# Row layout of the expert weights in SBUF: each partition's runs of 16 and 8 KB become runs of 8 and 4 KB

## The reference: what is computed

```python
x = x + merged @ w_out
return x + _moe(_rmsnorm(x, g_ffn), w_router, b_router, w_gu, b_gu, w_down, b_down)

# in _moe, for each block of tokens of expert e (top 4 of 32 experts per token):
hgu = tok[rows] @ w_gu[e] + b_gu[e]            # (tokens, 1024) @ (1024, 2048)
gate = jnp.minimum(hgu[:, 0::2], SWIGLU_LIMIT)
up = jnp.clip(hgu[:, 1::2], -SWIGLU_LIMIT, SWIGLU_LIMIT)
act = (up + 1.0) * (gate * jax.nn.sigmoid(SWIGLU_ALPHA * gate))
y = act @ w_down[e] + b_down[e]                # (tokens, 1024) @ (1024, 1024)
```

## Time and profile before

| | us |
|---|---|
| median of 3 runs | 1409.31 |
| lowest, highest | 1408.23, 1413.07 |
| the profiled execution | 1413.07 |
| its span, first to last instruction | 1411.3 |
| PE busy | 1320.6 (94%) |
| DVE busy, ACT busy | 282.4, 252.9 |
| DMA: moved, mean rate | 455.91 MB, 323 GB/s |

### The profile page before, as it was taken

The page is one execution under the profiler, slowest core; times in us unless marked ns, Lnnn a source line. Parts: engine busy times, 40 slices in busy tenths (PEclk is TensorE's granted clock), DMA queues, the critical chain, the costliest instruction groups (busy, mean ns, idle before and its releaser), DMA issues.

```text
span 1411.3 us, 15917 instructions
## 1 busy us (share of the span) xinstructions
PE 1320.6 (94%) x6068; PEld 623.2 (44%) x6069; DVE 282.4 (20%) x832; ACT 252.9 (18%) x515; POOL 24.7 (2%) x36
## 2 busy tenths in 40 slices
PE   5999999989969999999999999999999999999998
PEld 3574767877543343333333433333333333333332
DVE  2243434443141111111011111020111101111011
ACT  1115332344020111101101111011111110111111
POOL 2100000000000000000000000000000000000000
PEclk9999999999989999999999999999999999999999
DMA  9832137321398799995957999999999999999991
GB/s 317 316 123 90 60 132 279 127 71 68 119 360 369 327 425 427 423 427 221 388 231 304 427 426 424 427 426 426 427 423 426 426 427 427 424 425 428 427 420 79
DMA packets 63509, 455.91 MB, mean 323 GB/s; under 512 B 4964, under 2 KB 10232, under 8 KB 30680
## 3 DMA queue, kind: packets, MB, share of 16 engines
q1 hardware_dynamic: 62436, 453.50, 78.1%
q0 software_dynamic: 656, 1.46, 0.4%
q10 hardware_dynamic: 388, 0.55, 0.1%
HBM read 454.45 MB, written 1.05 MB: 323 GB/s over the span
## 4 chain that ended last, share of the span: by engine, by line
PE 54%; DMA 15%; ACT 2%; issue 1%; DVE 0%; SPq 0%; DVEq 0%; ACTq 0%
PE bank L930 26%; PE bank L960 15%; DMA ring<-in_w_down 15%; PE bank L901 4%; PE bank L917 3%; PE bank L893 3%; ACT mq L1222 1%; PE bank L949 1%; ACT sp_ L1212 1%; PE bank L987 0%; PE bank L848 0%; DVE sc L1603 0%; PE bank L836 0%; PE bank L874 0%; PE bank L878 0%
## 5 line engine op out<-in xcount | busy, mean ns | idle before, releaser
L930 PE MATMUL bank<-ring,sp_ 128*64 128x512 f32 x2176 | 481.1, 600 | 0.0
L930 PEld LDWEIGHTS bank<-ring,sp_ 128*64 128x64 f32 x2176 | 154.7, 138 | 324.1 <-issue 324.1
L960 PE MATMUL bank<-ring,mq 128*64 128x512 f32 x1088 | 245.8, 602 | 33.6 <-ACT mq L1222 24.5
L960 PEld LDWEIGHTS bank<-ring,mq 128*64 128x64 f32 x1088 | 76.9, 138 | 179.1 <-issue 154.7
L1646 DVE TENSOR_SCALAR sp_<-bank 128x256 f32<-128x256 f32 x68 | 28.6, 420 | 570.1 <-PE bank L930 570.1
L531 PE MATMUL bank<-ring 128*128 128x512 f32 x288 | 124.8, 593 | 3.1 <-DVE ring L1482 1.6
L1218 ACT ACTIVATE sp_<-sp_ 128x256 f32<-128x256 f32 x68 | 28.4, 418 | 510.1 <-DVE sp_ L1646 510.1
L652 PE MATMUL bank<-ring 128*128 128x256 f32 x448 | 99.4, 381 | 1.5 <-DVE sp_ L1493 1.5
L652 PEld LDWEIGHTS bank<-ring 128*128 128x128 f32 x448 | 84.2, 190 | 13.7 <-issue 2.5
L531 PEld LDWEIGHTS bank<-ring 128*128 128x128 f32 x288 | 54.4, 190 | 69.8 <-issue 67.7
L1662 DVE TENSOR_SCALAR sp_<-cst,rank_it,w_it 128x64 f32<-128x64 f32 x68 | 16.7, 312 | 280.5 <-PE bank L930 280.5
(11 more groups left out here) (289 smaller groups left out, 760.7 us busy)
## 6 DMA issues: line engine op xcount, KB each, us to landing
ring<-in_w_gu SPq DMA_DIRECT2D x128, 2048.0 KB, 25.0
ring<-in_w_down SPq DMA_DIRECT2D x64, 2048.0 KB, 16.4
ring<-in_w_in SPq DMA_DIRECT2D x13, 2048.0 KB, 11.4
ring<-in_w_mem_kv SPq DMA_DIRECT2D x2, 2048.0 KB, 10.1
ring<-in_w_out SPq DMA_DIRECT2D x2, 2048.0 KB, 8.9
ring<-in_cmp_w_k SPq DMA_DIRECT2D x1, 2048.0 KB, 8.2
ring<-in_cmp_w_v SPq DMA_DIRECT2D x1, 2048.0 KB, 9.2
ring<-in_w_br_mem SPq DMA_DIRECT2D x1, 2048.0 KB, 7.5
```

The costliest lines, as they stand in the source:

```text
L930: mm = nc.tensor.matmul(BH[b][64 * hh:64 * hh + 64, :], xgT[:, k, 64 * par:64 * par + 64], w[:, c, o:o + 512], start=False, stop=k == KT - ...
L960: mm = nc.tensor.matmul(BG[64 * hh:64 * hh + 64, :], actT[:, o:o + 64], w[:, c, 512 * hh:512 * hh + 512], start=k == 0, stop=k == KT - 1, ...
```

## The change

Both weight matrices are laid out in the plain way, row 128c+p on partition p. A chunk of `w_gu` becomes two runs of 8 KB per partition, a chunk of `w_down` four runs of 4 KB; either chunk is one contiguous stretch of 2 MB in HBM. `norm_row` then writes `x2` in its own order, and the transposes read neighbouring columns. Every chunk has the bytes, the slot, the semaphore and the place in SP's order that it had, and no matmul changes.

```diff
         def load_chunk(sp, e, q, odd):
             if q < 4:
-                n, src = 2, w_gu[e].rearrange("(p c) n -> p c n", p=P)[:, 2 * q:2 * q + 2, :]
+                n, src = 2, w_gu[e].rearrange("(c p) n -> p c n", p=P)[:, 2 * q:2 * q + 2, :]
             else:
-                n, src = 2, w_dn[e].rearrange("(c p two) n -> p c (two n)", p=P, two=2)[:, 2 * (q - 4):2 * (q - 4) + 2, :]
+                n, src = 4, w_dn[e].rearrange("(c p) n -> p c n", p=P)[:, 4 * (q - 4):4 * (q - 4) + 4, :]
...
                 for q in range(4):
-                    a = act_sb[:, 256 * (q // 2):256 * (q // 2) + 256].rearrange("p (f two) -> p f two", two=2)[:, :, q % 2]
-                    mm = nc.tensor.transpose(BX[:, P * q:P * q + P], a, ident)
+                    mm = nc.tensor.transpose(BX[:, P * q:P * q + P], act_sb[:, P * q:P * q + P], ident)
...
             def norm_row(i):
-                step(V.scalar_tensor_tensor(out=x2[:, i, :].rearrange("p (c d) -> p d c", c=KT),
-                                            in0=x_sb[:, i, :].rearrange("p (d c) -> p d c", c=KT),
-                                            scalar=st[:, 12 + i:13 + i], in1=g_ffn.rearrange("p (d c) -> p d c", c=KT),
+                step(V.scalar_tensor_tensor(out=x2[:, i, :], in0=x_sb[:, i, :], scalar=st[:, 12 + i:13 + i], in1=g_ffn,
                                             op0=ALU.mult, op1=ALU.mult), "x2_ready")
```

## The result

| | before | after |
|---|---|---|
| median, us | 1408.77 (4 runs, 1406.78 to 1413.07) | 1420.89 (4 runs, 1418.84 to 1421.86) |
| profiled execution: span, time | 1411.3, 1413.07 | 1418.2, 1419.95 |

The ratio is 1.0081 (95% interval 1.0059 to 1.0102). A second comparison on another occasion gave 1.0054 (1.0037 to 1.0070); the two intervals together reach from some 5 to 14 us. One execution of the kernel before in the second comparison took 2815.1 us and is not counted. The forecast was 1417, with a range of 1407 to 1423.

What follows compares the result with a forecast made beforehand. PE was taken to pace the work until 757 us, the unpausing DMA stream after that; +9.3 (packets) - 0.75 (norm_row) - 0.8 (transposes) = +7.7 us against the median 1409.31 gave 1417.0, range 1407 to 1423.

Steps and rivals of the forecast that it cites:

- the forecast's own case: Extra packets slow the expert weight stream, partly offset by cheaper norm_row and transposes: +7.7 us, 1412 to 1420, chance 0.56.
- the dearer rival: Expert weight stream: short packets cost what a lone 2 MB load shows, 0.80 us per expert, +14.4 us, 1423.7; chance 0.14.
- The stream sets the end, and only from 757 us on: Mixture of experts: PE paces until SP's last pause ends at 757.28 us, then the full DMA queue, 29.90 us per expert.
- 64 more packets, times a price, times 20 periods: Expert weight loads: 64 more packets per engine and expert at 7.3 ns, 0.47 us, over 20 periods: +9.3 us (0 to +16).
- The 2 KB row's 9.3 ns: Trunk loads of 2 KB runs at 387 GB/s: 9.3 ns per extra packet against 16 KB, used only as support.
- Hidden packets: Rival on the expert weight stream: overlap hides the extra packets, leaving only PE and DVE savings, -1.6 us, 1407.7; chance 0.20.
- Contiguous is faster: Rival: `w_gu` chunks, becoming contiguous in HBM, stream faster; at most 17.4 us, 1390.3 with savings, half-way 1399; chance 0.10.
- The lone load's rate: Rival: 4 KB runs stream at the 400 GB/s of a lone 2 MB load, 0.80 us per expert, 1423.7; chance 0.14.
- The check of the period: Packet times per expert sum to 29.5 us, plus 0.31 on the bias row's engine: 29.8 against the chain's 29.90.
- norm_row: DVE before the experts: unit steps cut the first call from 1.97 to 1.22 us, giving 0.75; the second call gives nothing.
- Transposes: PE weight loads fall from 207 to 142 ns: 0.065 us per item for 12 items before 757 us, 0.8 us (0 to 3.1).
- The signs to look for: Profile after: period about 30.4 us, rate 415 to 421, DMA waits before 1043.55, last pause's end within 3 us of 757.

## Why the prediction was right, and where it was off

- *The number.* 1420.89 lies in the range, but above the 1412 to 1420 that the forecast's own case was given, in the part that was there for the dearer rival. By the traces the change costs +12.2 - 1.4 = +10.8 us, where +7.7 was forecast; that the second comparison's ratio comes to +7.6 us is chance.
- *The stream sets the end, and only from 757 us on.* Shown, with one word to correct: the pause is the DMA engines' last, not SP's. T0 to T1 carries the loss in every trace but those of the shortest packets, which lose some before T0 too. T1 to the end is 42.2 to 43.8 us in the twelve traces, 43.8 before and 43.7 after; the five at 42.2 to 42.5 have TensorE at the lower clock for half as long there. In the kernel before, the slow last down-projection costs 9.97 - 7.29 = 2.7 us, not the 2.9 of the prediction.
- *64 more packets, times a price, times 20 periods.* The mechanism held; the price was the term that was mis-sized: 7.3 ns were forecast, 9.1 to 10.0 measured, so +12.2 us instead of +9.3. The 7.3 came from two rates that the windows give in whole GB/s: with 428 and 423 each off by half a unit, 612.5 and 309.9 ns move by 0.7 and 0.4, and two halves less a whole by 1.4; that a window cuts a few hundred packets comes on top. So rounding alone could hide a price of 8.7 ns. The 2 KB row's 9.3 ns, seven packets more against the same rounding (0.2 ns each), was the one to take; that it agrees to the tenth with the cut into 2 KB is partly luck. The estimate of 3.5 ns from the page "DMA: Bandwidth & Descriptors" of the Trainium skill (section "Why small descriptors are slow (HBM only)") is below what any of the six kernels shows (9.1 ns at the least).
- *Hidden packets* is excluded by the cut at unchanged addresses, 616.0 us for 610.2. *Contiguous is faster* is excluded by the run with only `w_gu` changed, whose chunks become contiguous: 616.1, as much as with the same number of packets at the old addresses. *The lone load's rate* (0.80 us per expert) is too dear: the period rose by 0.60.
- *The check of the period.* The prediction added up 29.5 us for the packets and 0.31 for the engine with the bias row, 29.8, close to 29.90. Spreading the row gave back 0.18, so this agreement was in part luck.
- *norm_row.* 1.28 us against a forecast of 1.22, so 0.69 and not 0.75 is given, and the second call's share did vanish in the wait for PE (1.00 us before L1625).
- *Transposes.* The weight loads fell to a median of 141 ns:

```profile
L948 PEld LDWEIGHTS bank<-cst,sp_ x136: 137/141/230, 435.5 to 1398.4; 128*128 128x128 f32 x136
```

The early items show what that is worth. Ten items of the kernel before take 733.53 - 450.70 = 282.83 us from up-projection to up-projection, ten of the kernel after 728.48 - 446.23 = 282.25, 0.06 us per item, as forecast. Below, rows of before and then after:

```profile
733.53 13.88 PE bank L930 x64
```

```profile
446.23 13.88 PE bank L930 x64
...
728.48 13.88 PE bank L930 x64
```

- *The signs to look for.* Rate 418 (415 to 421 was given), period 30.50 (about 30.4), waits from 952 us. One sign was badly set: a pause that ends more than 3 us elsewhere was to speak against the prediction, and it ended 5.1 us earlier. 3.8 of it came from the trunk, which the change does not touch. A moment that hangs on everything before it is no test; a distance between two events behind the change is.

What stays open: the comparisons of medians lie 3.4 us apart (+12.1 and +8.7 us) though T0 to T1 agrees within 0.3 us, and the +10.8 us of the traces lies above the second interval (5.2 to 9.9 us). Part of it is the granted clock. In the second comparison the 17 executions of the kernel before have a mean of 0.9846 and the ten of the kernel after 0.9859, and within one kernel the time falls by some 1.1 us for each 0.001 (before: 1416.29 us at 0.982, 1408.78 at 0.989). The means lie 8.4 us apart; at equal clock, an estimate, it would be 9.8. For the run with the loads alone the same working gives 10.4, against 12.2 between T0 and T1. The rest is not explained. The start of the mixture of experts moves by up to 8.5 us between traces with the trunk's clock; why the clock falls in one run's trunk and not in another's was not followed up.

## What to carry to other kernels

When weights stream without pause, count the packets per DMA engine, add a fixed price each (9.5 ns here, the time of some 250 bytes on one of 16 engines at 426 GB/s together), and look for the engine that carries something extra. In the kernel before, the sum over that engine's packets came within 0.1 us of the period, but not each of its terms did. Take such a price from the rows farthest apart in size, not from neighbours whose difference is at the rounding of the rates. To verify it, cut the packets at unchanged addresses, and measure between two events of the stream rather than by the whole time, in which noise from elsewhere was as large as half the effect. Where only whole times are at hand, compare executions with the same granted clock.

## What the runs showed of the hardware

- One more packet costs 9.1 to 10.0 ns whether 16, 8 or 4 KB are cut, although the DMA share of the windows is above 1 (1.01 to 1.05), which looks like room for overlap. A share above 1 did not mean that the cost of one more packet was covered.
- An issue on SP can take many microseconds while the stream is full. Durations of SP's issues of `w_gu` (ns, min/median/max) in the kernel before, after, and before with 16 KB cut in eight:

```profile
L350 SPq DMA_DIRECT2D ring<-in_w_gu x128: 327/345/1122, 312.0 to 1342.3; - x128
```

```profile
L350 SPq DMA_DIRECT2D ring<-in_w_gu x128: 367/389/9057, 310.8 to 1359.7; - x128
```

```profile
L350 SPq DMA_DIRECT2D ring<-in_w_gu x128: 367/1114/11731, 308.2 to 1391.5; - x128
```

The longest issue grows from 1.1 us to 9.1 and 11.7. It does not go by the number of packets alone: it is 10.4 us with only `w_down` changed and 4.0 with only `w_gu` changed, which add the same number, and 5.4 in the kernel after with every run halved again (9.9 for its issues of `w_down`). Here nothing else waits in SP's queue but loads that stand behind a full stream anyway, and the price per packet is the same with the long issues as without. In a kernel that issues small urgent transfers from the same queue they would wait.
- A landing follows the slowest of the engines, at least in part: taking one 8 KB packet per expert (0.31 us) off a single engine shortened the period of all of them by 0.18 us.
